# Layer norm of a gated convolution layer: applied on rows and transposed back, or on channels by spread statistics

## The reference, cut to what matters

```python
hn = x * rsqrt(mean(x * x) + 1e-6) * norm_g
a, b, gate = split(hn @ w_in, 3)                  # w_in 1024 x 3072
u = causal depthwise convolution of a * sigmoid(b), 31 taps, + conv_b
u = (u - mean(u)) * rsqrt(var(u) + 1e-5) * ln_g + ln_b     # over the 1024 channels
out = x + (silu(u) * silu(gate)) @ w_out          # w_out 1024 x 1024
```

## Time and profile before

| what | value |
|---|---|
| median of 3 runs | 374.76 us (374.57 to 375.19) |
| the profiled execution | 375.05 us |
| its span, first to last instruction | 373.3 us |
| PE busy | 368.0 us |
| DVE / POOL / ACT busy | 317.1 / 277.1 / 210.7 us |
| DMA moved | 39.32 MB |

### The profile page before, as it was taken

How to read it: one execution, slowest core, us unless ns; L and a number is a source line. 1 busy time by engine, 2 the same in 40 slices (tenths; PEclk the granted TensorE clock), 3 DMA queues, 4 the chain that set the end, 5 groups by cost and what they waited for, 6 DMA issues and landing times.

```text
span 373.3 us, 4921 instructions
## 1 busy us (share of the span) xinstructions
PE 368.0 (99%) x1664; PEld 299.0 (80%) x1664; DVE 317.1 (85%) x500; ACT 210.7 (56%) x319; POOL 277.1 (74%) x193
## 2 busy tenths in 40 slices
PE   7999999999999999999999999999999999999997
PEld 6888888888888888888888888888788888888886
DVE  4758799999998988999999999918457799999962
ACT  5879685558547633865666557732678653244000
POOL 0037999999999995999999999992773949273500
PEclk9999999999999999999999999999999999999999
DMA  7995011301111011111011111012447283620232
GB/s 262 400 404 186 14 56 59 112 6 51 56 58 57 1 58 56 56 58 56 17 43 56 56 58 31 28 56 79 154 162 266 97 313 108 233 98 15 97 142 101
DMA packets 13704, 39.32 MB, mean 105 GB/s; under 512 B 1520, under 2 KB 2032, under 8 KB 13680
## 3 DMA queue, kind: packets, MB, share of 16 engines
q1 hardware_dynamic: 13536, 38.87, 29.5%
q10 hardware_dynamic: 144, 0.15, 0.1%
HBM read 34.82 MB, written 4.19 MB: 105 GB/s over the span
## 4 chain that ended last, share of the span: by engine, by line
PE 97%; DMA 1%; SPq 0%; ACT 0%; DVE 0%; issue 0%
PE mm L540 66%; PE acc L628 12%; PE mm L628 9%; PE mm L557 6%; PE mm L608 2%; DMA nat<-x_t 1%; PE acc L619 1%; PE mm L619 1%; PE acc L534 0%; SPq L440 0%; ACT x_hi L688 0%; DVE nat L1124 0%; SPq L428 0%
## 5 line engine op out<-in xcount | busy, mean ns | idle before, releaser
L540 PE MATMUL mm<-x_hi,w_lo 128*128 128x512 f32 x352 | 140.3, 399 | 0.0
L540 PE MATMUL mm<-x_hi,w_hi 128*128 128x512 f32 x352 | 139.0, 395 | 0.0
L540 PE MATMUL mm<-x_lo,w_hi 128*128 128x512 f32 x352 | 138.8, 394 | 0.0
L1049 DVE SCALAR_TENSOR_TENSOR acc<-u,chan,acc 128x512 f32<-128x512 f32 x154 | 108.2, 747 | 0.1
L540 PEld LDWEIGHTS mm<-x_lo,w_hi 128*128 128x128 f32 x352 | 66.1, 188 | 16.6
L540 PEld LDWEIGHTS mm<-x_hi,w_hi 128*128 128x128 f32 x352 | 66.1, 188 | 15.3
L540 PEld LDWEIGHTS mm<-x_hi,w_lo 128*128 128x128 f32 x352 | 66.1, 188 | 15.3
L1303 POOL TENSOR_TENSOR pconv<-pconv,prod 128x512 f32<-128x512 f32 x60 | 77.4, 1315 | 0.0
L1049 DVE SCALAR_TENSOR_TENSOR acc<-u,w_sum,acc 128x512 f32<-128x512 f32 x90 | 67.2, 747 | 0.2
L777 ACT ACTIVATE prod<-u,chan 128x512 f32<-128x512 f32 x73 | 50.4, 718 | 13.0 <-POOL pconv L1303 11.2
L1249 POOL TENSOR_TENSOR w_lo<-raw,w_hi 128x1024 fp32r<-128x1024 f32 x21 | 50.8, 2420 | 8.9 <-ACT w_hi L727 8.7
(11 more groups left out here) (103 smaller groups left out, 527.6 us busy)
## 6 DMA issues: line engine op xcount, KB each, us to landing
raw<-w_in SPq DMA_DIRECT2D x22, 512.0 KB, 3.3
raw<-w_out SPq DMA_DIRECT2D x9, 512.0 KB, 3.3
nat<-x_t SPq DMA_DIRECT2D x16, 256.0 KB, 6.1
sgate<-x SPq DMA_DIRECT2D x8, 512.0 KB, 11.5
nat<-x SPq DMA_DIRECT2D x8, 512.0 KB, 6.0
y<-nat SPq DMA_DIRECT2D x15, 256.0 KB, 2.0
raw_late<-w_out SPq DMA_DIRECT2D x5, 512.0 KB, 3.4
sig<-w_out SPq DMA_DIRECT2D x4, 512.0 KB, 3.5
```

The source lines that it names most:

```text
L540: ins = nc.tensor.matmul(bank(("unit", m, h)), w[:, m % 3, k, :], xx[:, k, half(h)], start=(k == 0 and i == 0), stop=(k == KC - 1 and i == 2))
L1049: ins = nc.vector.scalar_tensor_tensor(dst, chain_in(j, chain, k), tap(j, chain, k), chain_bank(j, chain), ALU.mult, ALU.add)
```

## The change

Convolution outputs are written to `nat` with channels on the partitions (`y_part`) in place of `dconv` and `pconv`. The transposed copy goes to a small buffer `rows`, for the statistics alone. PE then spreads mean and `rstd` over the partitions by 16 small matmuls (`spread_mean`, `spread_rstd`: a column taken as a 128x128 weight, times identity), amid units (22, 0) and (22, 1). DVE subtracts the spread mean from each tile and half (`centre`, 16 instructions of 128x512), DVE (10) and POOL (6) multiply by the spread `rstd` (`scale`), ACT applies Silu from SBUF into a PSUM bank, and the gate follows. The 64 transposes of `transpose_norm`, the normalisation of the rows and `shift` are gone. Products 3, 4 and 6 go on accumulating in the PSUM banks of products 2, 0 and 5 (`CONTINUES`), which leaves 38 additions. Product 0 has q outside. Two "+11" sums and two lo parts of w_out move from POOL to DVE (`add_11`, `finish_wb_lo`). Banks, waits and the order of all queues follow.

```diff
-                   (19, 0): [(4, 0), (4, 1)]}
+                   (20, 0): [(4, 0), (4, 1)]}
...
-STATS_AT = {12: [0], 14: [1], 20: [2]}
-NORM_AT = {(23, 1): ((0, 1), (1, 1), (2, 1))}
-NORM_IN_FIRST = ((3, 4, 5), (6, 7), (), ())
+STATS_AT = {10: [0], 14: [1], 19: [2]}
+MEAN_SPREAD_AT = {(22, 0, 3): 0, (22, 0, 7): 1}
+RSTD_SPREAD_AT = {(22, 0, 7): 0, (22, 1, 2): 1}
+POOL_SCALES = {0: (1, 3, 5, 7), 1: (1, 3)}
...
+CONTINUES = {3: 2, 4: 0, 6: 5}
+ADDS = (("11",), ("11",), ("22",), ("21",), ("21", "12", "22"), ("22",), ("12",))
...
+            if b == 6 and q >= TPH - 1:
+                return acc[:, q - TPH + 1, 0:HALF // 2]
+            if q >= 2:
+                return mm[:, LEFT[q - 2], :] if b in (0, 4) else acc[:, q, :]
+            if b == 1:
+                return acc[:, 2 + q, :]
+            return acc[:, q, :] if b in (0, 4) else mm[:, FREE[q], :]
...
+            def spread_mean(h):
+                pe.wait_ge(mv_ready, TPH * (h + 1))
+                for i in range(TPH):
+                    ins = nc.tensor.matmul(norm_spread(h, 0)[:, i * P:(i + 1) * P],
+                                           mean_var[:, TPH * h + i, 0:1].to_broadcast([P, P]), ident[:],
+                                           start=True, stop=True)
...
             def out_product(b):
...
+                    elif b == 1:
+                        pe.wait_ge(post_done, POST[1, "11", q - 2])
...
+            def act_norm(k, h):
+                act.wait_ge(z_pool if k in POOL_SCALES[h] else z_dve, Z_COUNT[k, h])
+                wait_bank(act, ("gated", k, h))
+                nc.scalar.activation(by_parity(bank(("gated", k, h))), y_half(k, h), ACT.Silu, ...)
...
+            def centre(k, h):
+                dve.wait_ge(mean_spread, h + 1)
+                nc.vector.tensor_tensor(y_half(k, h), y_half(k, h), by_parity(norm_spread(h, 0)),
+                                        ALU.subtract).then_inc(y_centred, 1)
...
             def load_x(h):
-                sp.wait_ge(nt_ready, KC * (h + 1))
                 for t in range(TPH * h, TPH * (h + 1)):
+                    sp.wait_ge(actv_ready, KC + t + 1)
                     sp.dma_start(nat[:, t, :], x[t * P:(t + 1) * P, :]).then_inc(x_in[t], 16)
```

More of the change, by code:

```diff
@@ L238, in gated_conv_layer @@
         vlo_ready = sem("vlo_ready")
+        spare_in = [sem(f"spare_in{i}") for i in range(2)]
         wo_in = [[sem(f"wo_in{which}{i}") for i in range(2)] for which in "ab"]
@@ L241, in gated_conv_layer @@
         wb_done = sem("wb_done")
+        wb_late = sem("wb_late")
         vsum_ready = sem("vsum_ready")
@@ L258, in gated_conv_layer @@
             JOBS += [("conv", *jh) for jh in CONV_TRANSPOSES.get((m, h), [])]
[L259 to L266, removed]
+        TURN = {job: n % 4 for n, job in enumerate(JOBS)}
+        LATE = [("unit", m, h) for m, h in PASSES if m >= NU - 2]
+        for n, job in enumerate(LATE):
+            TURN[job] = TURN[LATE[n % 2]]
+        GATED = [("gated", k, h) for h in range(NH) for k in range(KC)]
+        FREE = [bank for bank in range(4) if bank not in (TURN[LATE[0]], TURN[LATE[1]])]
+        for n, job in enumerate(GATED):
+            TURN[job] = FREE[n % 2]
+        BANK, EARLIER, LAST = TURN, {}, {}
+        for job in JOBS + GATED:
             EARLIER[job] = LAST.get(BANK[job])
@@ L270, in gated_conv_layer, with y_half, by_parity, y_part @@
         CT = {jh: n + 1 for n, jh in enumerate(CONV_JOBS)}
-        ALT = [BANK["norm", k, 1] for k in range(CK, KC)]
+        CONV_ORDER = [j for j, h in CONV_JOBS if h == 0]
+        DVE_SCALES = [(k, h) for h in range(NH) for k in range(KC) if k not in POOL_SCALES[h]]
+        Z_COUNT = {(k, h): sum(len(POOL_SCALES[i]) for i in range(h)) + POOL_SCALES[h].index(k) + 1
+                   for h in range(NH) for k in POOL_SCALES[h]}
+        Z_COUNT.update({kh: n + 1 for n, kh in enumerate(DVE_SCALES)})
+        LEFT = [BANK[LATE[2]], BANK[LATE[3]]]
+        def y_half(k, h):
+            return nat[:, k, :].rearrange("p (s n) -> p s n", s=2)[:, :, Q * h:Q * (h + 1)]
+        def by_parity(columns):
+            return columns.rearrange("p (s q) -> p s q", s=2)
+        def y_part(j, parity):
+            return nat[:, j, parity * HALF:(parity + 1) * HALF]
+        def norm_spread(h, what):
+            return acc[:, 2 * h + what, :]
+        def rstd_row(h):
+            return rows[:, 2 * h:2 * h + 2, :].rearrange("p t c -> p (t c)")
         def w_raw(which, i):
@@ L499, in _ @@
                 load_w_out("b", i, 0, 0)
+            sp.wait_ge(unit_ready["g"], NH * KC)
+            for i in range(2):
+                sp.dma_start(spare[:, i, :].rearrange("p (k n) -> p k n", k=2), w_out[0, 2 + i]).then_inc(spare_in[i], 16)
             load_x(0)
[L501 to L503 removed]
             load_x(1)
             for i in range(2):
[L506 removed]
+                sp.wait_ge(wb_late, W_BY_VECTOR["+11", 4, i])
                 load_w_out("b", i, 1, 0)
@@ L574, in transpose_middle @@
             def transpose_middle(m, h):
[L576 to L580, removed]
+                for _, j, of in MID_TRANSPOSES.get((m, h), ()):
+                    transpose_conv(j, of)
             def project(m, h):
@@ L628, in product_terms @@
                     ins = nc.tensor.matmul(product_bank(b, q), v[:, k0 + k, rows], w[:, k, piece_columns(b, q)],
-                                           start=(k == 0 and i == 0), stop=(k == CK - 1 and i == 2))
+                                           start=(k == 0 and i == 0 and continued(b, q) is None),
+                                           stop=(k == CK - 1 and i == 2),
+                                           skip_group_check=continued(b, q) is not None)
                 if k == CK - 1:
@@ L659, in _ @@
                     transpose_conv(*jh)
[L660 to L672, removed]
+            for b in range(7):
                 out_product(b)
@@ L799, in split_w_out, with copy_rstd @@
                 nc.scalar.activation(w_pair(b, i)[0], w_source(b, i), ACT.Copy).then_inc(wb_hi, 1)
[L801 to L806, removed]
+            def copy_rstd(h):
+                act.wait_ge(rstd_spread, h + 1)
+                nc.scalar.activation(rstd_row(h), norm_spread(h, 1), ACT.Copy).then_inc(rstd_copied, 1)
             def act_norm(k, h):
-                n = KC * h + k
-                act.wait_ge(nt_ready, n + 1)
-                nc.scalar.activation(bank(("norm", k, h)), bank(("norm", k, h)), ACT.Silu, scale=ln_g[:, k:k + 1],
+                act.wait_ge(z_pool if k in POOL_SCALES[h] else z_dve, Z_COUNT[k, h])
+                wait_bank(act, ("gated", k, h))
+                nc.scalar.activation(by_parity(bank(("gated", k, h))), y_half(k, h), ACT.Silu, scale=ln_g[:, k:k + 1],
                                      bias=ln_b[:, k:k + 1]).then_inc(actv_ready, 1)
@@ L1117, in post @@
                 tile = min(q, TPH - 1)
-                earlier = EARLIER_ADD[b, part]
+                earlier = EARLIER_ADD[b, part, q]
                 if earlier is None:
@@ L1121, in post, with posts @@
                 else:
-                    dve.wait_ge(post_done, POST[earlier, part, tile])
+                    dve.wait_ge(post_done, earlier)
                 total = out_part(part, tile, piece_columns(b, q))
                 nc.vector.tensor_tensor(total, product_bank(b, q), total, ALU.add).then_inc(post_done, 1)
-            def posts(b):
+            def posts(b, columns=range(TPH + 1)):
                 for post_b, part, q in POSTS:
-                    if post_b == b:
+                    if post_b == b and q in columns:
                         post(b, part, q)
@@ L1184, in _ @@
             for h in range(NH):
+                take_stats(KC // 2 - 1, range(TPH * h, TPH * (h + 1)))
                 moments(h)
-                normalise(h)
             for k in range(KC):
-                gate(k, 0)
+                centre(k, 0)
             for k in range(KC):
-                split_v(k // CK, k % CK)
-            for k in range(CK + 2):
+                scale(k, 0)
+            gate(0, 0)
+            gate(1, 0)
+            for k in range(CK):
+                centre(k, 1)
+            gate(2, 0)
+            gate(3, 0)
+            for k in range(CK):
+                scale(k, 1)
+            for k in range(CK, KC):
+                centre(k, 1)
+            for k in range(CK):
+                split_v(0, k)
+            for k in range(CK):
+                gate(CK + k, 0)
+            for k in range(CK, KC):
+                scale(k, 1)
+            gate(0, 1)
+            gate(1, 1)
+            for k in range(CK):
+                split_v(1, k)
+            for k in range(2, KC):
                 gate(k, 1)
@@ L1194, in _ @@
                 sum_v(2, k)
-            for k in range(CK + 2, KC):
-                gate(k, 1)
+            posts(1, (0,))
             for k in range(CK):
                 split_v(2, k)
+            posts(1, (1,))
+            for i in range(2):
```

(18 more changed lines are left out.)

234 lines of the change are left out of this document (133 added, 101 removed), and 2 rows, old and new, of the table W_OPS.

## The result

370.29 us, median of 4 runs (370.11 to 370.56), against 374.9 us before (374.57 to 375.19): a ratio of 0.9882 (95% interval 0.9869 to 0.9894), 4.6 us less. Both kernels were timed anew for this; the first set of the kernel before had a median of 374.76 us. The forecast was 371.3 us and a gain of 3.4 us. The direction was right, the size was 1.2 us too small.

A forecast was written before the change was run, and what follows sets the result against it. PE's instruction list was taken to bound the kernel: 6.99 us off and 3.56 us on shorten the 373.3 us span by 3.43 to 369.9; plus 1.75 minus 0.29 gives 371.3 us, range 370.7 to 373.5.

The forecast's parts named there:

- PE's list is the kernel's time: PE works without waiting on other engines from 8 to 370.5 us, so a change pays by what it takes off PE.
- What goes from PE, what PE gets: 64 transposes at line 619 go, 6.99 us; 16 small float32 spread matmuls come, 3.56 us; PE's list 3.43 us shorter.
- the rival of dear spreads: Spread matmuls cost 0.39 us each, 6.3 us against 6.99, giving 374.1 us; chance 0.08, shared with stalls eating the whole gain.
- Up to 258 us at nothing: Moved tile 4 transposes and DVE statistics before 258 us cost nothing; without cover at DVE's wait for POOL, 2.7 us at most.
- products that lose nothing: Output products keep 7 x 48 matmuls of 128x512, 11.24 us each; going on in a bank saves additions, not matmuls.
- From span to time: Whole execution: span 369.9 us, plus 1.75 us outside it, minus 0.29 us from profiled execution to median, gives 371.3 us.
- From 258 us on: Hand layout of the entry to the products: product 0 starts at 288.36 us, no wait on PE, least margins about 1.5 us.
- the small stalls: Rival at the entry to the products: handovers use up the margins, PE waits 0.5 to 2 us, 372.5 us; chance 0.22.
- first `sum_v` ending near 301: Sign to look for on DVE; the prediction's layout instead had `sum_v(2)` run from 300.4 to 302.8 us.
- The shared bank: Rival in product 1: tile 2 waits about 5 us for tile 0's addition, 376.5 us; chance 0.08, including another such wait.
- The point at which the change stops paying: At product 1's shared bank: the change stops paying above 3.43 + 1.8 us of delay, gain plus margin.
- The 19 additions: Additions saved on DVE, 11.6 us, count only as slack and more than pay for four w_out operations moved there.

The follow-up runs named there:

- e3: The kernel before with each of its 64 transposes of normalised rows issued twice; 382.6 us, ratio 1.020 to before.
- e4: The changed kernel with each of its 16 spread matmuls issued twice; 374.09 us, 3.8 us more than the changed kernel.
- e1: The changed kernel with the unused 32 bytes a partition of `shift` still allocated, so later buffers keep their old addresses; 371.82 us, ratio to before 0.9915.
- e2: The kernel before with `shift` allocated behind all other tensors, so the weights' buffers lie at the new addresses; 373.57 us, ratio 0.9958.
- e7: The changed kernel with eight extra DVE additions ahead of the one that releases the bank for product 1's third tile; 376.08 us, ratio 1.0023.
- e8: The changed kernel with 19 extra DVE additions into a scratch tensor (12 with product 0, 4 with product 2, 3 with product 5); 375.89 us, ratio 1.0018.
- e9: The kernel before with padding alone, so that nat, x_hi, x_lo, w_hi, w_lo and the wb tensors begin at multiples of 2048 bytes; 366.94 us.

## Why the prediction was right in its parts and wrong in its size

- *PE's list is the kernel's time.* Right; shown by both chains and by e3 and e4.
- *What goes from PE, what PE gets.* Right in both sizes, 6.99 and 3.56 us in the chains. The repeated column costs nothing extra, 0.89 us a call, so the rival of dear spreads fell.
- *Up to 258 us at nothing, and products that lose nothing, "11.24 us a product, as before".* This is the step that failed. The order of work was read rightly: no wait of PE came or went. But both terms took the distance between matmuls as given. It fell, which was worth 0.90 us up to 258 us and 0.42 behind it (a product takes 11.20 us). The change moves the weights' buffers by 32 bytes, and e1 and e2 show that this is worth 1.3 to 1.5 us over the kernel. No row of the trace of before could show it; the diff could, and I read the removal of `shift` as a tensor gone, not as addresses moved. Without this effect the forecast would have stood: e1, at the old addresses, takes 371.82 us.
- *From span to time.* The 1.75 us between them was taken over and is 2.11 us in the changed kernel, and the profiled execution was taken as 0.29 us above the median and lies 0.18 below. Together that is 0.8 us the other way. So the span was missed by 1.9 us (368.0 against 369.9), the time by only 1.0, and that it is so close is in part luck; so are the 0.5 us by which this execution began its work earlier.
- *From 258 us on.* The layout by distances between starts held on thirty instructions in a row to within 0.7 us, and no wait of PE appeared, so the small stalls did not cost anything. The new subtractions, with one input in PSUM, ran beside POOL as the row promised: four took 2.47 us from 274.10 us, while POOL worked on w_out. The sign "first `sum_v` ending near 301" came true (300.99 us), but it did not agree with the layout's own 302.8.
- *The shared bank.* It did not decide, but e7 shows that it is real: its margin is 2.0 us in the trace (1.8 forecast). The point at which the change stops paying was put too far off. It is not 3.43 + 1.8 us of delay on a clock that stays, since the clock's fall costs as much again as most of the wait. The rule of the Trainium skill (TensorE: Matmul & The Clock Gate, Part 1) that an idle TensorE falls to its lower level was weighed there without a row. The profiled executions of e7 and e8 agree: granted clock 0.50 behind 3.7 us of idleness, 0.57 behind 3.1.
- *The 19 additions.* Right that they are only slack, and e8 shows that the slack is needed.

What stays open: why the distance depends on that difference. e2's products run at 232.3 ns and the changed kernel's at 233.3 with w_out's buffers at the same addresses, 0.3 us that placement alone does not explain. Differences of 32, 64, 96 and 224 bytes were not run in the projection. Also open is what takes the 0.3 us outside the span.

## What to carry to other kernels

Where one engine's list is the time, a change is priced by what it takes off that list, and each of the other engines needs a margin that is written down. But a diff also has effects that are in no instruction: whatever it allocates or frees moves all that lies behind it. So compare the distance between like instructions in the untouched stretches first, and repeat the change at the old addresses before crediting it with the whole. Padding can then be worth more than the change itself: here 8 us against 3.4. A wait that leaves the bounding engine idle for some us has to be priced with the work behind it, at the lower clock.

## What the runs showed of the hardware that was not expected

- In the projection the distance between fp32r matmuls of 128x512 with a weight load each was 226.8, 228.9, 232.4 or 233.4 ns at 2.4 GHz, with the weights 0, 192, 128 or 160 bytes (modulo 256) above the activations in the partition. In the products, where the roles of the two are swapped, it was 226.7 ns at 0, 233.3 at 192, 232.3 to 233.3 at 128 and 234.2 at 160. From one end to the other that is 6.6 ns in the projection (2.9%) and 7.5 in the products; on 1152 and 348 matmuls an estimate is 10 us. The kernel before gained 8 us by padding alone (e9, 374.9 to 366.94 us), with one wait of 1.0 us on POOL that came with it.
- After 3.7 us of idleness TensorE's granted clock stood at 0.50 for four us (e7), and the 24 matmuls there took 1.5 times as long. After 3.1 us (e8) it was 1.3 times, at 0.57 for four us.
